# The memory's key and value blocks planned at every fourth step of NSA's attends, not at every third

## The reference, cut to what matters

```python
o_gla = gla_mixer(gq, gk, gv, gr, glr, ...)
o_nsa = nsa_mixer(nq, kc, vc, ks_, vs_, kw, vw, ng, rel_bias, ...)   # 3 branches: compressed, selected, window
h = h + jnp.concatenate([o_gla, o_nsa], axis=-1) @ w_out[l]
h = h + cross_attn(rms_norm(h, norm_xattn[l]), rms_norm(mem, norm_mem[l]), xa_wq, xa_wk, xa_wv, xa_wo)

def cross_attn(hn, memn, wq, wk, wv, wo):
    k = (memn @ wk).reshape(B, M, XA_HEADS, XA_DH)      # the memory's keys: they need nothing of h
    v = (memn @ wv).reshape(B, M, XA_HEADS, XA_DH)      # the memory's values: nor do they
    ...
```

## The kernel before, in words

| n | PE work planned at its start | n | PE work planned at its start |
|---|---|---|---|
| 0 | scores of b0 and of an attend of tile 0 | 19 | transposes of b1 |
| 4 | their transposes | 21, 22 | outputs of tile 0, group 1, in two halves; at 22 also transposes of one attend of tile 1 |
| 6 | scores of two attends of tile 0 | 24 | scores of two attends of tile 1 |
| 10 | their transposes | 28 | their transposes |
| 12, 13 | outputs of tile 0, group 0, in two halves; at 12 also scores of tile 0's last attend | 30, 31 | outputs of tile 1, group 0; at 30 also scores of the last attend |
| 15, 16 | scores of b1; transposes of tile 0's last attend | 34 | its transposes |
| 18 | scores of tile 1's first attend | 37, 38 | the last outputs, tile 1, group 1 |

## Time and profile before

### The profile page before, as it was taken

One profiled execution on the slowest core, in us unless ns is written; L12 is line 12 of the kernel. 1 busy time (PEld: TensorE's weight loads), 2 busy tenths in 40 slices (PEclk: granted clock), 3 DMA queues, 4 the chain that ended last, 5 costly groups with the idle time before them and its releaser, 6 DMA issues.

```text
span 2529.7 us, 39068 instructions
## 1 busy us (share of the span) xinstructions
PE 2371.8 (94%) x15354; PEld 2140.0 (85%) x15354; DVE 1661.3 (66%) x3195; ACT 1342.1 (53%) x2494; POOL 775.1 (31%) x404
## 2 busy tenths in 40 slices
PE   6878998999999999998888988999999999999998
PEld 5876888999999888887857876789999999888886
DVE  4564456977778566665667475666977788566665
ACT  3344444468888444554533454244458888444443
POOL 3000002877776000000800053101887777000000
PEclk8888899999999999999999998999999999999999
DMA  5322324655555566564332343245555455556653
GB/s 176 124 93 68 99 94 150 176 176 166 163 164 169 189 191 192 191 192 134 117 125 84 125 135 109 67 150 159 182 176 161 166 162 164 184 191 192 192 192 123
DMA packets 108286, 383.36 MB, mean 152 GB/s; under 512 B 12975, under 2 KB 15840, under 8 KB 107528
## 3 DMA queue, kind: packets, MB, share of 16 engines
q1 hardware_dynamic: 108104, 380.86, 47.1%
HBM read 379.74 MB, written 1.06 MB: 151 GB/s over the span
## 4 chain that ended last, share of the span: by engine, by line
PE 80%; DVE 11%; ACT 4%; DMA 2%; issue 2%; POOL 0%; SPq 0%; DVEq 0%; ACTq 0%; POOLq 0%
PE psum L370 23%; PE psum L372 22%; PE psum L371 22%; PE psum L2031 2%; PE psum L402 2%; DVE weight_parts L343 2%; ACT weight_parts L338 2%; PE psum L607 1%; PE psum L2696 1%; PE psum L2476 1%; PE psum L1457 1%; PE psum L1018 1%; PE psum L1358 0%; DVE hg_tmp L1064 0%; PE psum L1780 0%
## 5 line engine op out<-in xcount | busy, mean ns | idle before, releaser
L349 POOL TENSOR_TENSOR weight_parts<-weight_ring,weight_parts 128x1024 fp32r<-128x1024 f32 x276 | 670.4, 2440 | 507.8 <-ACT weight_parts L338 507.4
L370 PE MATMUL psum<-acts_high,weight_parts 128*128 128x256 f32 x2744 | 793.2, 289 | 23.0 <-DVE weight_parts L343 11.1
L372 PE MATMUL psum<-acts_high,weight_parts 128*128 128x256 f32 x2744 | 781.5, 285 | 0.0
L371 PE MATMUL psum<-acts_low,weight_parts 128*128 128x256 f32 x2744 | 780.9, 285 | 0.0
L338 ACT ACTIVATE weight_parts<-weight_ring 128x1024 fp32r<-128x1024 f32 x674 | 710.3, 1055 | 127.9 <-PE psum L372 60.1
L343 DVE TENSOR_TENSOR weight_parts<-weight_ring,weight_parts 128x1024 fp32r<-128x1024 f32 x398 | 488.1, 1228 | 292.5 <-ACT weight_parts L338 292.0
L370 PEld LDWEIGHTS psum<-acts_high,weight_parts 128*128 128x128 f32 x2744 | 531.2, 194 | 34.8 <-issue 13.0
L371 PEld LDWEIGHTS psum<-acts_low,weight_parts 128*128 128x128 f32 x2744 | 531.3, 194 | 1.4 <-issue 0.5
L372 PEld LDWEIGHTS psum<-acts_high,weight_parts 128*128 128x128 f32 x2744 | 531.1, 194 | 0.0
L370 PE MATMUL psum<-weight_parts,peer_coef 128*128 128x512 f32 x1024 | 401.3, 392 | 4.0 <-issue 3.9
L372 PE MATMUL psum<-weight_parts,peer_coef 128*128 128x512 f32 x1024 | 403.0, 394 | 0.0
(11 more groups left out here) (426 smaller groups left out, 3143.0 us busy)
## 6 DMA issues: line engine op xcount, KB each, us to landing
weight_ring<-in_peer_down SPq DMA_DIRECT2D x128, 512.0 KB, 3.5
weight_ring<-in_peer_up SPq DMA_DIRECT2D x128, 512.0 KB, 3.5
weight_ring<-in_peer_u SPq DMA_DIRECT2D x128, 512.0 KB, 3.5
weight_ring<-in_peer_v SPq DMA_DIRECT2D x128, 512.0 KB, 3.5
weight_ring<-in_w_in SPq DMA_DIRECT2D x88, 512.0 KB, 3.6
weight_ring<-in_w_out SPq DMA_DIRECT2D x16, 512.0 KB, 3.4
weight_ring<-in_peer_w_q SPq DMA_DIRECT2D x16, 512.0 KB, 3.6
weight_ring<-in_w_in_v SPq DMA_DIRECT2D x10, 512.0 KB, 3.5
```

The lines of the kernel that those rows point to most:

```text
L349: q.e.tensor_tensor(self.low, self.ring, self.high.bitcast(F32), ALU.subtract).then_inc(*self.unit.ready.once())
L370: q.e.matmul(out, sh, mh, start=first, stop=False)
L371: q.e.matmul(out, sh, ml, start=False, stop=False)
L372: return q.e.matmul(out, sl, mh, start=False, stop=last)
```

## The change

The loop over NSA's steps asks the memory's stream for its next block at every fourth turn and not at every third:

```diff
             for n, _ in enumerate(nsa(c, inner, s, nq, kv, vt, o[:, 4:8, :], s.attended, s.attended, room)):
                 if n in (2, 4, 6, 8):
                     c.plan(SplitActs(c, o[:, n // 2 - 1, :], xn, n // 2 - 1, room))
-                if n % 3 == 0 and streaming:
+                if n % 4 == 0 and streaming:
                     if next(streaming, "over") == "over":
                         streaming = None
                         c.flush(c.dram["w_out"][0], c.dram["w_out"][1])
```

## The result

The changed kernel takes 2541.51 us, the median of 22 runs, against 2534.74 us, the median of 22 runs of the kernel before on the same chips. The ratio is 1.0026 with a 95% interval of 1.0016 to 1.0036: slower by 6.6 us, 4.1 to 9.1. Forecast was +6.5. One of the changed kernel's 22 runs took 4661.66 us; it counts as slow, the ratio and its interval leave it out, and nothing here explains it. The profiled execution took 2533.64 us, its span 2531.8. The profiled one of before took 2531.52, so the two profiles lie only 2 us apart, and both are under their kernel's median. That alone says that something in the time differs from one execution to the next.

What follows compares the result with a forecast made beforehand. PE's gaps and half clock in NSA's stretch were taken to bound the kernel. Gaps of +6.3 and clock of +0.2 summed to +6.5 us, 2538.7 us against the median of 2532.2; range 2530.5 to 2546.5.

Steps and rivals of the forecast that it cites:

- What bounds: PE runs without a gap from 282 us on, so NSA's stretch passes its gain or loss to the kernel's end.
- n = 0 to 6: First transposes' gap grows by K6's 2.9 us, the next scores' gap becomes 1.45 instead of 0.52; +3.8 us.
- n = 6 to 10: Between scores and transposes K7 alone covers, leaving a gap of 4.0 us where 2.53 was; +1.5 us.
- n = 12 to 22: V1 and V2 cover the attends' copies, closing gaps of 0.69 and 1.23; V4's split may add 0.3; -1.6 us.
- n = 24 to 28: Only V3 lies between scores and transposes, its copies ahead of the exponentials; a new gap, largest term, +4.8 us.
- n = 28 to 38: V4 to V7 cover copies and part of the last chain; changes of -0.4, -0.6 and -1.2, sum -2.2 us.
- The gaps together: Sum of PE's gap changes over all turns: +6.3 us, together +4 to +8.
- The clock: Half-clock changes: +3.2 early, -1.0 over light work, +3.2 at n = 28, -5.2 in the tail; +0.2 us.
- B: Rival: clock falls at both new gaps and stays low in the tail; +12.7 us, 2544.9 us; chance 0.21.
- A: Rival: no clock drop at the two new gaps, tail's gain stays; +0.1 us, 2532.3 us; chance 0.20.
- C: Rival: V3's copy holds exponentials less, gap at n = 28 is 1.6, no drop; -3.1, 2529.1 us; chance 0.05.
- D: Rival: blocks fall out of the loop and run behind the last outputs; 2541.9 us; chance 0.04.

Runs made afterwards that it cites:

- K6 at 4: The kernel before with product K6 (and V0's split) planned at n = 4, not 3; 2537.04 against 2535.11 us, ratio 1.0009.
- V3's copies late: The changed kernel with the value blocks' copies out of PSUM planned at n = 26, behind the exponentials, not n = 24; ratio to before 1.0015.
- both kernels with added matmuls: Matmuls nobody reads, added in the changed kernel's three long gaps (ratio to before 1.0015) and in the tail of the kernel before (0.9980).
- the kernel with added matmuls: The changed kernel with matmuls nobody reads added at n = 3, 9 and 27, in its three long gaps; ratio to before 1.0015.
- K5 at 3, K7 at 9: The kernel before with K5 planned at n = 3, not 0, and K7 at 9, not 6; 2518.89 us, ratio 0.9940.
- best order: The kernel before with K5 to V7 at n = 3, 3, 9, 9, 13, 16, 20, 25, 27, 33, 36; 2508.51 us, ratio 0.9900.

## Why the prediction was right, and where it wasn't

- **What bounds.** Right: the stretch's end is passed on. In the three profiles of each kernel what follows the stretch took 2247.8, 2252.6 and 2252.6 us before, and 2247.8, 2252.4 and 2251.7 after, with no part of the change in it. But it took 2246.0 to 2252.6 us over all 14 profiles, so executions also differ by up to 6.6 us in what the change doesn't touch.
- **n = 0 to 6, +3.8.** 5.15 and 1.42 against 5.1 and 1.45. Right, and shown alone by K6 at 4.
- **n = 6 to 10, +1.5.** Mis-sized: 4.49 and 0.35 us, which is +2.3. The first exponential began 2.36 us after the scores, where the sum has 1.85 for scores, bias and maximum. On DVE a split of activations (L797) stood ahead of the bias until 203.68, 0.3 us after the 0.85 of scores in the sum (DVE's row, then ACT's):

```profile
203.25 0.43 DVE L797 TENSOR_TENSOR acts_low<-mix_o,acts_high 128x256 fp32r<-128x256 f32 x1 [5.72 <-ACT acts_high L793]
```

```profile
204.85 0.40 ACT L1417 ACTIVATE nsa_s<-nsa_s,nsa_max 128x128 f32<-128x128 f32 x1 [1.63 <-DVE nsa_max L1396]
```

  And I let one gap stand for two: the second attend's transposes wait for their own normalizing when the first run at full clock.
- **n = 12 to 22, -1.6.** Right: 0.69 and 1.23 gone, 0.37 come.
- **n = 24 to 28, +4.8.** 4.80 and 0.27. Right in size. V3's copies late shows the cause for 2.3 of the 5.07: the copies ahead of the exponentials; the rest is the lost cover.
- **n = 28 to 38, -2.2.** 1.91 left of 4.38, -2.5. Right. The splits of `w_out` 0 and 1, costed at nothing, did cost nothing: no gap stands ahead of `w_out`'s first matmul.
- **The gaps together:** 19.5 for 12.3, +7.2 against 6.3.
- **The clock, +0.2.** This is the term that was mis-sized most, and the mechanism was right in part. What the half clock cost at each place (half of the work at 1.2 GHz, in us), in the three profiles of each kernel, summed over windows of some 0.2 us:

| place | before | after | difference of the means | forecast |
|---|---|---|---|---|
| K5's beginning | 2.9, 1.5, 3.0 | 1.4, 2.7, 1.5 | -0.6 | 0 |
| behind the first gap, n = 4 | 0, 4.9, 0 | 1.8, 2.7, 1.8 | +0.5 | +3.2 |
| n = 10 | 5.0, 5.0, 5.0 | 4.9, 5.9, 5.0 | +0.2 | 0 |
| over light work, n = 15 to 22 | 3.3, 0, 3.4 | 0, 3.3, 0 | -1.1 | -1.0 |
| n = 28 | 0, 0, 0 | 1.6, 2.2, 1.6 | +1.8 | +3.2 |
| tail | 5.8, 4.3, 4.3 | 0, 0, 0 | -4.8 | -5.2 |

  So the drops fell where they were forecast. But those behind the two long gaps were 1.6 to 2.7 us each where I took 3.2, and before had, in one profile of three, a drop of its own at n = 4, which the one trace that I read from didn't show. The sum is -4 in these profiles, against +0.2; against the mean of before, the single profiles of after give -6, -6 and +1.
- **The total.** That +6.5 meets +6.6 is luck: the gaps were 0.9 over the forecast, the clock in the profiles 4 under it. The stretch was 3.3 us longer in the mean of the three profiles (97.2 and 100.5), and the ratio of all runs says 4.1 to 9.1. With gaps of +7.2, that ratio puts the clock's mean part between -3 and +2, if nothing else changed; three profiles don't settle it, and it stays open.
- **Rivals.** B's tail at half clock wasn't seen, nor A's gaps without a drop. C, a gap of under 2 us behind V3, and D, blocks that fall out of the loop, didn't occur. B's +12.7 left out the -1.0 over light work that A and C keep; with it B was +11.7.
- **The page on the clock.** "TensorE: Matmul & The Clock Gate" of the Trainium skill, section "Loop structure matters more than you think", has the clock fall by long waits between matmuls. The drops behind gaps of 4.5 us and more agree, and so do both kernels with added matmuls. The drops at 226.90 in after's second profile (6.70 us) and at 221.20 in the kernel with added matmuls, with a gap of 0.78 ahead, are not covered by that section.

## What to carry to other kernels

Work that only fills another chain's waits should be placed by which wait it covers, and not by an even step: list the chain's waits for each turn, and put one filler in each, two where the wait is long. Then look at what each filler hangs on a second engine's queue (here its copy out of PSUM and the split of a block further on), since that stands in order ahead of the chain's own next step, and plan it behind. On TensorE a closed gap may pay twice, by its length and by the clock over what follows (here behind gaps of 2.3 to 5.2 us, though not behind each), so count both, and take the clock's part from several executions.

## What the runs showed of the hardware that was not expected

- With nothing else ahead of it on ACT, the load of an activation table (1.28 us) went at 179.17 (K5 at 3, K7 at 9), 8 us before the first exponential had its input, and so it did in the best order. In before it was planned behind a copy that waited for PE; it went at 189.70, behind the copy and right ahead of the exponential.
- Of the 26 us that the best order gains in this stretch, 16 come from the clock in the two profiles: 34.8 us of work at 1.2 GHz became 2.9.
- The same program did 19.9 and 34.4 us of its stretch's work at 1.2 GHz in two executions, with idle times of 19.3 and 18.8 us.
- Behind the gap ahead of the first transposes the clock fell for 9.8 us of work in one execution of before (gap of 2.32 us), and stayed up in two others (2.19 and 2.09 us).
